# Split matrix products that stream the columns of each moving tile in chunks of 16, taken in turn from its two halves

## The chip, the cores and the metric

The kernel runs on one core of one Trainium2 chip. The metric is the device time of one execution in microseconds. Of the kernel before there are three timed runs, 2678.69, 2678.70 and 2680.71 us, so its median is 2678.7 us. One further execution was recorded by the hardware profiler; it took 2682.11 us, of which 2680.3 us lie between its first and its last instruction (its span). All rows below are of that execution.

## What is computed

Two transformer blocks in fp32, on 512 latent tokens (and 256 context tokens in the first block) of width 1024. Cut to the dense products, which are what the change touches:

```python
# first block, once
hx = modulate(rms_norm(x), sh1, sc1); hc = modulate(rms_norm(ctx), csh1, csc1)
... = split_cols(hx @ w_in)                  # 1024 x 7712; the context takes its first 3616 columns
... attention over 768 keys; a gated delta rule in both directions over chunks of 64 ...
x = x + g1 * ((sigmoid(g_a) * (attn @ w_pa) + sigmoid(g_d) * (gdn @ w_pd)) @ w_out)
x = x + g2 * conv_ffn(...)                   # w_up 1024 x 5632, w_down 2816 x 1024
# second block, twice
proj = rms_norm_2(h, norm1_g[l]) @ w_in[l]   # 1024 x 2576
... pool mixer, differential attention, gated linear attention ...
h = h + mix @ w_out[l]
h = h + square(relu(rms_norm_2(h, norm2_g[l]) @ w_mlp1[l])) @ w_mlp2[l]   # 1024 x 4096 x 1024
return rms_norm_2(h, final_norm_g)
```

## The kernel before

**Layout.** Activations lie with the feature on the partition and the token along the row: `KD` = 8 tiles of 128 features, each 512 columns wide (`LAT`) or 768 (`TOK`, with the context). A product gives 128 output features by 512 tokens, which fill one bank of PSUM, in fp32.

**Split products.** Each dense product is made of three products of "fp32r" operands, a high part and the rest: high x high, low x high and high x low. So a weight unit of 8 x 128 rows by 128 columns gives 24 TensorE matmuls into one bank, each with a weight load (LDWEIGHTS) of its own and a moving operand of 512 columns. Three pieces of code issue them. `product` (L321) streams the activations and holds the weights; for 768 tokens it issues two matmuls for each step, of 512 and of 256 columns. `product_tok` (L331) holds a tile of activations and streams the weights, 256 or 512 columns. `part` in `stage_mixer` (L2696) is `product` cut so that other work can go between. In the rows, `ps<-u_hi,w_lo` names the moving operand first and the stationary one behind it; the tiles `u`, `mid`, `h`, `h_lat`, `src`, `attn_back` and `gdn_o` are such pairs.

**Other TensorE work.** Attention, the delta rule, transposes and the small mixers use plain fp32 matmuls. The compiler makes two instructions of one such matmul; the table and the rows count instructions.

**Weights.** SyncE loads units of 512 KB into a ring of 4 in the order of their use (`stream_weights`). ScalarE copies a unit to `w_hi` (L291), VectorE subtracts it from the unit into `w_lo` (L299), two slots each. TensorE's `unit()` waits for `w_lo`; `unit_used` gives a slot back.

**Order.** Each stage has one hand-written program per engine, in a fixed order. TensorE works a product's unit from k = 0 to 7 in one go and turns over four banks (`n % 4`), so that ScalarE and VectorE can empty one while the next is filled.

**Alignment.** A tile of 512 elements or more starts at a multiple of 512 bytes in its row (`ROW`); so does the weight tile of each k, which is 128 columns of 4 bytes.

Of the kernel before, what the change touches and what calls it, by code (L numbers as in the profile page):

```python
# [25 lines left out]
P = 128  # L26
# [21 lines left out]
NCH = LAT // GLA_C  # L48
RING = 4
ROW = 512  # L50
UNIT = 8 * P
MOD_FIRST = 16
BIG = -1.0e30
# [109 lines left out]
def build(nc, t_vecs, t_mats, t_tabs, t_rope, t_x, t_w, out):  # L163

    with ExitStack() as top:
        signals = {}

        def sig(name):
            if name not in signals:
                signals[name] = Signal(top.enter_context(nc.semaphore(name)))  # L170
            return signals[name]
# [13 lines left out]
        def start_of(shape):  # L185

            return ROW if int(np.prod(shape)) >= ROW else 32

        def sb(ctx, name, *shape):

            taken[name] = taken.get(name, 0) + 1
            name = name if taken[name] == 1 else f"{name}_{taken[name]}"
            return ctx.enter_context(nc.sbuf_tensor(name, [P, *shape], F32, align_bytes=start_of(shape)))

        def sbr(ctx, name, *shape):
            taken[name] = taken.get(name, 0) + 1
            name = name if taken[name] == 1 else f"{name}_{taken[name]}"
            return ctx.enter_context(nc.sbuf_tensor(name, [P, *shape], F32R, align_bytes=start_of(shape)))

        def far_pair(ctx, name, *shape):  # L200

            taken[name] = taken.get(name, 0) + 1
            return tuple(ctx.enter_context(nc.sbuf_tensor(f"{name}_{part}{taken[name]}", [P, *shape], F32R, side="right",
                                                          align_bytes=ROW))
                         for part in ("hi", "lo"))
# [6 lines left out]
        mod = sb(top, "mod", 48, 2)  # L212
        ring = sb(top, "ring", RING, UNIT)
        w_hi, w_lo = sbr(top, "w_hi", 2, UNIT), sbr(top, "w_lo", 2, UNIT)
        tabs = sb(top, "tabs", NTAB)
        vecs = sb(top, "vecs", NVEC)
        ps = top.enter_context(nc.psum_tensor("ps", [P, 8, 512], F32))
# [84 lines left out]
        def unit(pe):  # L302

            n = at["used"]
            at["used"] += 1
            if whole[n]:
                pe.wait_ge(loaded[n % RING], 16 * (n // RING + 1))
                return ring[:, n % RING, :]
            pe.wait_ge(lo_ok.sem, n_split[n] + 1)
            return w_hi[:, n_split[n] % 2, :], w_lo[:, n_split[n] % 2, :]  # L310

        def pair(n):
            return ps[:, 2 * (n % 4):2 * (n % 4) + 2, :].rearrange("p b n -> p (b n)")

        def product(pe, w, src, dst, n_tok, k0=0, nk=KD, start=True, stop=True):

            for k in range(nk):
                for wi, xi in ((0, 0), (0, 1), (1, 0)):
                    for a, b in ((0, min(n_tok, LAT)), (LAT, n_tok)):
                        if a < b:  # L320
                            mm = nc.tensor.matmul(dst[:, a:b], w[wi][:, k * P:(k + 1) * P],  # L321
                                                  src[xi][:, k0 + k, a:b], start=start and k == wi == xi == 0,
                                                  stop=stop and k == nk - 1 and wi == 1)
            return mm

        def product_tok(pe, w, src, dst_of, n_tiles, cols, k0=0, nk=KD, start=True, stop=True):

            for t in range(n_tiles):
                for k in range(nk):
                    for xi, wi in ((0, 0), (0, 1), (1, 0)):  # L330
                        mm = nc.tensor.matmul(dst_of(t), src[xi][:, k0 + k, t * P:(t + 1) * P],  # L331
                                              w[wi][:, k * cols:(k + 1) * cols],
                                              start=start and k == wi == xi == 0,
                                              stop=stop and k == nk - 1 and xi == 1)
            return mm
# [13 lines left out]
        def stage_modulation(x, h, scratch, sq_scratch, spare):  # L349
# [22 lines left out]
            with stage_block() as block:  # L372
# [60 lines left out]
                def _(pe):  # L433
# [38 lines left out]
                    for k in range(KD):  # L472
                        pe.wait_ge(*h_low.at(k + 1))
                        mm = product(pe, tuple(p[:, k * P:(k + 1) * P] for p in w), h, pair(0), TOK, k0=k, nk=1,
                                     start=k == 0, stop=k == KD - 1)
# [127 lines left out]
        def product_of_norm(pe, w, src, dst, first=1):  # L603

            low = sig("norm_low")
            for k in range(KD):
                pe.wait_ge(*low.at(k + first))
                mm = product(pe, tuple(p[:, k * P:(k + 1) * P] for p in w), src, dst, LAT, k0=k, nk=1,
                             start=k == 0, stop=k == KD - 1)
            return mm  # L610
# [30 lines left out]
        def stage_attn_inputs(h, q, kk, vtok, spare, t1, rope, q_ss):  # L641
# [9 lines left out]
            with ExitStack() as s:  # L651
                sq, root = (spare[:].rearrange("p t n -> p (t n)")[:, a * 2 * TOK:(a + 1) * 2 * TOK]
                            .rearrange("p (b n) -> p b n", b=2) for a in range(2))
                with stage_block() as block:
# [6 lines left out]
                    def _(pe):  # L661
                        pe.wait_ge(*sig("tabs_rest").at(0))
                        for a in range(2):
                            w = unit(pe)
                            product_tok(pe, w, h, lambda t: ps[:, 2 + t, 0:KV_HEADS * P], TT, KV_HEADS * P, k0=4 * a,
                                        nk=4, start=a == 0, stop=a == 1).then_inc(*unit_used.one())
                        for n in range(n_items + 2):
                            if 0 < n < n_items:
                                w = unit(pe)
                                pe.wait_ge(*evac.at(max(n, 2)))  # L670
                                product(pe, w, h, pair(n % 2), items[n][1]).then_inc(*unit_used.one())
# [1897 lines left out]
        def stage_mixer(layer, u, x, first_gain, rstd, mats, mix):  # L2569
# [37 lines left out]
            def bank(n):  # L2607
                return n if n < 3 else (n - HEAD) % 2
# [18 lines left out]
            with ExitStack() as s:  # L2627
# [33 lines left out]
                with stage_block() as block:  # L2661
# [27 lines left out]
                    def _(pe):  # L2689
                        def part(w, n, k0, k1):  # L2690

                            for k in range(k0, k1):
                                if n == 0:
                                    pe.wait_ge(*sig("norm_low").at(k + 1 - KD))
                                for wi, xi in ((0, 0), (0, 1), (1, 0)):
                                    mm = nc.tensor.matmul(ps[:, bank(n), :], w[wi][:, k * P:(k + 1) * P], u[xi][:, k, :],  # L2696
                                                          start=k == wi == xi == 0, stop=k == KD - 1 and wi == 1)
                            if k1 == KD:
                                mm.then_inc(*unit_used.one())
# [107 lines left out]
                        for n in range(3):  # L2807
                            w = unit(pe)
                            pe.wait_ge(*evac.at(n - 3))
                            part(w, n, 0, KD)  # L2810
                            if n == 0:
                                pe.wait_ge(*lam_ok.at(1))
                                nc.tensor.matmul(ps[:, 7, 0:2], ones, lam[:, 0:2], start=True,
                                                 stop=True).then_inc(*lams_ok.one())
                        pe.wait_ge(*rs_ok.at(1))
                        for t in range(TL):
                            mm = nc.tensor.transpose(ps[:, 3, t * P:(t + 1) * P], rstd[:, t * P:(t + 1) * P], ident)
# [3 lines left out]
                                         start=True, stop=True).then_inc(*p_ok.one())  # L2821
                        pe.wait_ge(*lame_ok.at(1))
                        for i in range(2):
                            w = unit(pe)
                            product_tok(pe, w, u, lambda t: ps[:, 4 + t, 0:256], TL, 256,
                                        k0=4 * i, nk=4, start=i == 0, stop=i == 1).then_inc(*unit_used.one())
                        pe.wait_ge(*evac.at(3))
                        pe.wait_ge(*rc_ok.at(1))
                        for i in range(4):
                            w = unit(pe)  # L2830
                            for t in range(TL):
                                if i == 0 and t > 1:
                                    pe.wait_ge(*tok_evac.at(t - 1))
                                mm = product_tok(pe, w, tuple(a[:, :, t * P:(t + 1) * P] for a in u),
                                                 lambda _: ps[:, (2, 3, 6, 7)[t], :], 1, 512, k0=2 * i, nk=2,
                                                 start=i == 0, stop=i == 3)
                            mm.then_inc(*unit_used.one())
                            if i == 1:
                                pe.wait_ge(*d_ok.at(9))
                                for t in range(TL):  # L2840
                                    mm = nc.tensor.transpose(ps[:, 0, t * P:(t + 1) * P], ke[:, t * P:(t + 1) * P], ident)
# [6 lines left out]
                            elif i == 3:  # L2848
                                pe.wait_ge(*d_ok.at(11))
                                gla_states()  # L2850
                        pe.wait_ge(*d_ok.at(13))
                        part(unit(pe), HEAD, 0, KD)
                        w = unit(pe)
                        part(w, HEAD + 1, 0, 2)
                        pe.wait_ge(*d_ok.at(20))
                        pe.wait_ge(*tok_evac.at(8))
                        gla_out()
                        part(w, HEAD + 1, 2, KD)
                        for s in range(SLOTS):
                            n = FIRST + s  # L2860
                            ending, starting = items_ending(s), items_starting(s)
                            w = unit(pe)
# [472 lines left out]
        with ExitStack() as s:  # L3335
# [37 lines left out]
            u = far_pair(normed, "u", KD, LAT)  # L3373
# [8 lines left out]
            for layer in range(DEPTH2):  # L3382
                with ExitStack() as s2:
# [4 lines left out]
                    u = far_pair(normed, "u", KD, LAT)  # L3388
# [135 lines left out]
```

## Time and profile before

| | us |
|---|---|
| median of 3 runs | 2678.7 |
| profiled execution | 2682.1 |
| its span | 2680.3 |
| PE (matmul) busy | 2577.4 |
| PEld (weight load) busy | 2081.2 |
| VectorE busy | 1399.7 |
| ScalarE busy | 1023.4 |
| GpSimd busy | 277.2 |

A matmul's recorded time holds its way through the array as well as its streaming, and neighbours overlap: one of 512 columns is shown with 0.39 us while the next starts 0.23 us behind it. What a matmul costs in a dense run is therefore read from start to start. The granted clock is 1.00 for 2.4 GHz and 0.50 for 1.2 GHz; its mean in this execution is 0.975.

### The profile page before, as it was taken

Reading aid. Unit: us, or ns where it says so; the run is one execution under the profiler, and the core shown is the slowest. Engines: PE = TensorE matmul, PEld = TensorE weight load, DVE = VectorE, ACT = ScalarE, POOL = GpSimd, SP = SyncE. Lnnn points to the kernel's source line nnn. Section 1 sums busy time; section 2 is a strip of 40 time slices with the busy share of each in tenths; the row PEclk is TensorE's granted clock in tenths of the full one; section 3 lists DMA queues with packets and bytes.
Section 4 is the critical chain, followed back from the end, with each engine's and each line's share of the span. In section 5 each row is a group of like instructions: output and inputs, shape, how many; then the busy total and the mean of one; then the engine's idle time right before and its main releaser. Section 6 shows DMA issues by size and latency. Waiting matters only on the chain.

```text
span 2680.3 us, 46124 instructions
## 1 busy us (share of the span) xinstructions
PE 2577.4 (96%) x19758; PEld 2081.2 (78%) x19758; DVE 1399.7 (52%) x1950; ACT 1023.4 (38%) x1697; POOL 277.2 (10%) x228
## 2 busy tenths in 40 slices
PE   6998999999998999899999999999999999999998
PEld 5755787778987788688888877788888876788887
DVE  4345698545677433566653546553453446552542
ACT  3245665423334322333333436432233346431222
POOL 0210102223331000111101001100001001100001
PEclk8999999979999999999999989999999999999999
DMA  6100310131003233222323211233232211223322
GB/s 263 57 16 20 114 56 33 65 128 66 4 4 134 86 101 104 101 95 95 98 93 100 87 56 48 79 102 95 95 101 96 87 48 48 95 94 99 98 95 71
DMA packets 64715, 222.91 MB, mean 83 GB/s; under 512 B 7168, under 2 KB 7552, under 8 KB 64384
## 3 DMA queue, kind: packets, MB, share of 16 engines
q1 hardware_dynamic: 63936, 218.39, 24.3%
q8 instruction: 157, 2.57, 0.4%
q10 hardware_dynamic: 576, 1.57, 0.1%
q14 instruction: 46, 0.38, 0.0%
HBM read 213.64 MB, written 6.29 MB: 82 GB/s over the span
## 4 chain that ended last, share of the span: by engine, by line
PE 89%; DVE 6%; issue 2%; ACT 2%; DMA 1%; POOL 0%; SPq 0%; POOLq 0%; DVEq 0%; ACTq 0%
PE ps L321 59%; PE ps L2696 6%; PE ps L1715 5%; PE ps L331 3%; PE ps L837 2%; PE ps L812 1%; PE ps L1721 1%; PE ps L1740 1%; PE ps L1757 1%; DMA ring<-in_w_mod_first 1%; PE ps L2747 1%; DVE w_lo L299 1%; PE ps L828 1%; PE ps L2777 1%; PE ps L1915 1%
## 5 line engine op out<-in xcount | busy, mean ns | idle before, releaser
L299 DVE TENSOR_TENSOR w_lo<-ring,w_hi 128x1024 fp32r<-128x1024 f32 (+1 forms) x339 | 420.7, 1241 | 835.3 <-ACT w_hi L291 835.2
L291 ACT CAST w_hi<-ring 128x1024 fp32r<-128x1024 f32 (+1 forms) x339 | 353.9, 1044 | 922.1 <-PE ps L321 832.2
L321 PE MATMUL ps<-u_hi,w_hi 128*128 128x512 f32 x864 | 338.7, 392 | 9.0 <-DVE u_lo L580 9.0
L321 PE MATMUL ps<-u_hi,w_lo 128*128 128x512 f32 x864 | 336.9, 390 | 0.0
L321 PE MATMUL ps<-u_lo,w_hi 128*128 128x512 f32 x864 | 336.9, 390 | 0.0
L321 PE MATMUL ps<-mid_hi,w_hi 128*128 128x512 f32 x688 | 267.6, 389 | 0.0
L321 PE MATMUL ps<-mid_lo,w_hi 128*128 128x512 f32 x688 | 267.6, 389 | 0.0
L321 PE MATMUL ps<-mid_hi,w_lo 128*128 128x512 f32 x688 | 267.6, 389 | 0.0
L321 PEld LDWEIGHTS ps<-u_hi,w_hi 128*128 128x128 f32 x864 | 162.5, 188 | 46.8 <-issue 8.9
L321 PEld LDWEIGHTS ps<-u_hi,w_lo 128*128 128x128 f32 x864 | 162.6, 188 | 34.0
L321 PEld LDWEIGHTS ps<-u_lo,w_hi 128*128 128x128 f32 x864 | 162.6, 188 | 33.8 <-issue 0.5
L2371 POOL TENSOR_TENSOR project_acc<-project_acc,project_sq 128x512 f32<-128x512 f32 x42 | 54.0, 1292 | 1140.2 <-ACT project_sq L2392 1140.2
L321 PEld LDWEIGHTS ps<-mid_hi,w_lo 128*128 128x128 f32 x688 | 129.1, 188 | 26.9
L321 PEld LDWEIGHTS ps<-mid_hi,w_hi 128*128 128x128 f32 x688 | 129.1, 188 | 26.8
L321 PEld LDWEIGHTS ps<-mid_lo,w_hi 128*128 128x128 f32 x688 | 129.1, 188 | 26.8
L321 PE MATMUL ps<-h_hi,w_hi 128*128 128x512 f32 (+1 forms) x432 | 139.5, 380 | 3.7 <-ACT gdn_v L709 2.6
L321 PE MATMUL ps<-h_lo,w_hi 128*128 128x512 f32 (+1 forms) x432 | 129.3, 357 | 0.3 <-issue 0.3
L321 PE MATMUL ps<-h_hi,w_lo 128*128 128x512 f32 (+1 forms) x432 | 128.9, 356 | 0.0
L2696 PE MATMUL ps<-u_hi,w_hi 128*128 128x512 f32 x240 | 104.2, 434 | 0.0
L2696 PE MATMUL ps<-u_hi,w_lo 128*128 128x512 f32 x240 | 95.7, 399 | 0.0
L2696 PE MATMUL ps<-u_lo,w_hi 128*128 128x512 f32 x240 | 95.3, 397 | 0.0
L321 PEld LDWEIGHTS ps<-h_hi,w_hi 128*128 128x128 f32 x432 | 72.2, 191 | 22.2 <-DVE w_lo L299 5.9
(449 smaller groups left out, 4677.5 us busy)
## 6 DMA issues: line engine op xcount, KB each, us to landing
ring<-in_w_up SPq DMA_DIRECT2D x44, 512.0 KB, 3.4
ring<-in_w_in SPq DMA_DIRECT2D x42, 512.0 KB, 3.5
ring<-in_w_merge SPq DMA_DIRECT2D x32, 512.0 KB, 3.5
ring<-in_w_mlp1a SPq DMA_DIRECT2D x32, 512.0 KB, 3.5
ring<-in_w_mlp2a SPq DMA_DIRECT2D x32, 512.0 KB, 3.5
ring<-in_w_mlp1b SPq DMA_DIRECT2D x32, 512.0 KB, 3.5
ring<-in_w_mlp2b SPq DMA_DIRECT2D x32, 512.0 KB, 3.5
ring<-in_w_gdn_in SPq DMA_DIRECT2D x24, 512.0 KB, 3.5
```

What stands on the lines that cost most here:

```text
L291: nc.scalar.copy(w_hi[:, slot, 0:width], ring[:, n % RING, 0:width]).then_inc(*hi_ok.one())
L299: nc.vector.tensor_tensor(w_lo[:, slot, 0:width], ring[:, n % RING, 0:width], as_f32(w_hi[:, slot, 0:width]), ALU.subtract).then_inc(*lo_o ...
L321: mm = nc.tensor.matmul(dst[:, a:b], w[wi][:, k * P:(k + 1) * P], src[xi][:, k0 + k, a:b], start=start and k == wi == xi == 0, stop=stop a ...
L331: mm = nc.tensor.matmul(dst_of(t), src[xi][:, k0 + k, t * P:(t + 1) * P], w[wi][:, k * cols:(k + 1) * cols], start=start and k == wi == xi ...
L812: mm = nc.tensor.matmul(pair(i % 2)[:, a:b], q[:, h, t * P:(t + 1) * P], kk[:, h // GROUP, a:b], start=True, stop=True)
L828: mm = nc.tensor.transpose(pt_bank[:, k * P:(k + 1) * P], pr[:, i % 2, k * P:(k + 1) * P], ident)
L837: mm = nc.tensor.matmul(ps[:, 6, :], vtok[:, k, c:c + P], pt[:, k, :], start=k == 0, stop=k == TT - 1)
L1715: mm = nc.tensor.matmul(dst[:, h * P:(h + 1) * P], lhs(h), rhs(h), start=True, stop=True)
L1721: mm = nc.tensor.transpose(dst[:, h * P:(h + 1) * P], src(h), ident)
L1740: mm = nc.tensor.matmul(packed(y_bank(d)[r, h * B32 // 2:(h + 1) * B32 // 2], 2 << lev), n_block(n, d, h, r, r), joined(up[r, d, h * B32:( ...
L2371: nc.gpsimd.tensor_tensor(acc[:, i, :], acc[:, i, :], sq[:, i, n % 2, :], ALU.add).then_inc(*add_ok.one())
L2696: mm = nc.tensor.matmul(ps[:, bank(n), :], w[wi][:, k * P:(k + 1) * P], u[xi][:, k, :], start=k == wi == xi == 0, stop=k == KD - 1 and wi ...
```

## The change

```diff
+LINE = 16
...
+        def halves(a):
+            return a.rearrange("p (half l c) -> p l half c", half=2, c=LINE)
+
         def product(pe, w, src, dst, n_tok, k0=0, nk=KD, start=True, stop=True):
...
-                            mm = nc.tensor.matmul(dst[:, a:b], w[wi][:, k * P:(k + 1) * P],
-                                                  src[xi][:, k0 + k, a:b], start=start and k == wi == xi == 0,
+                            mm = nc.tensor.matmul(halves(dst[:, a:b]), w[wi][:, k * P:(k + 1) * P],
+                                                  halves(src[xi][:, k0 + k, a:b]), start=start and k == wi == xi == 0,
...
-                        mm = nc.tensor.matmul(dst_of(t), src[xi][:, k0 + k, t * P:(t + 1) * P],
-                                              w[wi][:, k * cols:(k + 1) * cols],
+                        mm = nc.tensor.matmul(halves(dst_of(t)), src[xi][:, k0 + k, t * P:(t + 1) * P],
+                                              halves(w[wi][:, k * cols:(k + 1) * cols]),
...
-                                    mm = nc.tensor.matmul(ps[:, bank(n), :], w[wi][:, k * P:(k + 1) * P], u[xi][:, k, :],
+                                    mm = nc.tensor.matmul(halves(ps[:, bank(n), :]), w[wi][:, k * P:(k + 1) * P],
+                                                          halves(u[xi][:, k, :]),
```

The moving operand of a 512-column matmul was read as columns 0 to 511. Now it is read as 0-15, 256-271, 16-31, 272-287 and so on, 32 chunks; one of 256 columns as 0-15, 128-143, 16-31 and so on, 16 chunks. The output goes to the same columns of PSUM in the same order, so each sum lands where it did. The stationary operand, its load, the number and order of the instructions, waits, DMAs and all other engines are as before.

TensorE, at the border of the projection behind the first block's merge and the stage of `w_up` (`src` and `u` are split activations, `project_acc` and `project_sq` sums for a norm), before:

```order
L321 MATMUL ps<-src_hi_buf,w_hi 128x512
L321 MATMUL ps<-src_lo_buf,w_hi 128x512
L321 MATMUL ps<-src_hi_buf,w_lo 128x512
L2358 MATMUL ps<-project_acc,tabs 128x512
L2361 MATMUL ps<-project_sq,tabs 128x512
L2489 UNCONDITIONAL_BRANCH
L321 MATMUL ps<-u_hi,w_hi 128x512
L321 MATMUL ps<-u_lo,w_hi 128x512
L321 MATMUL ps<-u_hi,w_lo 128x512
```

and now:

```order
L325 MATMUL ps<-src_hi_buf,w_hi 128x16x2x16
L325 MATMUL ps<-src_lo_buf,w_hi 128x16x2x16
L325 MATMUL ps<-src_hi_buf,w_lo 128x16x2x16
L2362 MATMUL ps<-project_acc,tabs 128x512
L2365 MATMUL ps<-project_sq,tabs 128x512
L2493 UNCONDITIONAL_BRANCH
L325 MATMUL ps<-u_hi,w_hi 128x16x2x16
L325 MATMUL ps<-u_lo,w_hi 128x16x2x16
L325 MATMUL ps<-u_hi,w_lo 128x16x2x16
```

The split matmuls read 16 x 2 x 16 columns where they read 512; the two plain ones and the order stand as they were (the lines are four further down).

TensorE, in `product_tok` of the mixer of the second block, where the moving operand is the weights, before:

```order
L331 MATMUL ps<-w_hi,u_hi 128x256
L331 MATMUL ps<-w_lo,u_hi 128x256
L331 MATMUL ps<-w_hi,u_lo 128x256
L331 MATMUL ps<-w_hi,u_hi 128x512
L331 MATMUL ps<-w_lo,u_hi 128x512
L331 MATMUL ps<-w_hi,u_lo 128x512
```

and now:

```order
L335 MATMUL ps<-w_hi,u_hi 128x8x2x16
L335 MATMUL ps<-w_lo,u_hi 128x8x2x16
L335 MATMUL ps<-w_hi,u_lo 128x8x2x16
L335 MATMUL ps<-w_hi,u_hi 128x16x2x16
L335 MATMUL ps<-w_lo,u_hi 128x16x2x16
L335 MATMUL ps<-w_hi,u_lo 128x16x2x16
```

Here too only the shape is another: 8 x 2 x 16 for 256 columns, 16 x 2 x 16 for 512.

## Rows read from the trace of the kernel before

**Rows 1.** The page: engines' busy time, and the chain by engine and by line.

```profile
PE 2577.4 (96%) x19758; PEld 2081.2 (78%) x19758; DVE 1399.7 (52%) x1950; ACT 1023.4 (38%) x1697; POOL 277.2 (10%) x228
...
PE 89%; DVE 6%; issue 2%; ACT 2%; DMA 1%; POOL 0%; SPq 0%; POOLq 0%; DVEq 0%; ACTq 0%
PE ps L321 59%; PE ps L2696 6%; PE ps L1715 5%; PE ps L331 3%; PE ps L837 2%; PE ps L812 1%; PE ps L1721 1%; PE ps L1740 1%; PE ps L1757 1%; DMA ring<-in_w_mod_first 1%; PE ps L2747 1%; DVE w_lo L299 1%; PE ps L828 1%; PE ps L2777 1%; PE ps L1915 1%
```

**Rows 2.** The chain in order of time: start us, us, what (long pieces).

```profile
1138.15 355.48 PE ps L321 x1566
...
1612.73 1.39 PE ps L2696 x6
...
1733.24 348.22 PE ps L321 x1536
```

**Rows 3.** Busy PE in the whole span of L321, L331, L2696: us, us (count), clock.

```profile
0.00:2681.00 2681.00, 1687.33 (x7488) 0.98 0.25 83
...
0.00:2681.00 2681.00, 85.71 (x528) 0.98 0.25 83
...
0.00:2681.00 2681.00, 188.65 (x720) 0.98 0.25 83
```

**Rows 4.** Groups by form: the three products of `h` have 256-column forms, 152 each.

```profile
L321 PE MATMUL ps<-h_hi,w_hi 128*128 128x256 f32 x152 | 43.1, 283 | 0.0
...
L331 PE MATMUL ps<-w_hi,u_hi 128*128 128x512 f32 x64 | 25.3, 396 | 0.0
```

**Rows 5.** Timeline of PE, full clock: start us, us, engine, line, operation.

```profile
1859.82 0.39 PE L321 MATMUL ps<-mid_lo,w_hi 128*128 128x512 f32 x1
...
1865.94 0.39 PE L321 MATMUL ps<-mid_lo,w_hi 128*128 128x512 f32 x1
```

**Rows 6.** The same, at half clock, shortly after a wait.

```profile
1690.87 0.63 PE L321 MATMUL ps<-src_hi_buf,w_lo 128*128 128x512 f32 x1
...
1692.58 0.63 PE L321 MATMUL ps<-src_hi_buf,w_hi 128*128 128x512 f32 x1
```

**Rows 7.** The same, plain fp32 at full clock: a run cut after 5 and after 7; L1715.

```profile
179.44 2.41 PE L837 MATMUL ps<-o_tok,gdn_v 128*128 128x512 f32 x5 [0.89 <-ACT o_tok L881]
...
179.44 3.27 PE L837 MATMUL ps<-o_tok,gdn_v 128*128 128x512 f32 x7 [0.89 <-ACT o_tok L881]
...
646.93 1.06 PE L1715 MATMUL ps<-gdn_St,gdn_k 128*128 128x128 f32 x8
```

**Rows 8.** All of L837: ns min/median/max, first and last start.

```profile
L837 PE MATMUL ps<-o_tok,gdn_v x96: 592/592/697, 164.7 to 272.0; 128*128 128x512 f32 x96
```

**Rows 9.** Timeline: 256 columns alone, and 512 and 256 in pairs (x2).

```profile
58.04 0.28 PE L331 MATMUL ps<-w_lo,h_hi 128*128 128x256 f32 x1
...
58.76 0.28 PE L331 MATMUL ps<-w_lo,h_hi 128*128 128x256 f32 x1
...
351.50 0.51 PE L321 MATMUL ps<-h_hi,w_lo 128*128 128x512 f32 x2
...
352.54 0.51 PE L321 MATMUL ps<-h_hi,w_lo 128*128 128x512 f32 x2
...
411.61 0.51 PE L321 MATMUL ps<-h_hi,w_lo 128*128 128x512 f32 x2
...
415.85 0.40 PE L321 MATMUL ps<-h_hi,w_lo 128*128 128x512 f32 x1
```

**Rows 10.** Groups by form: small matmuls of 16 columns each, mean ns of one.

```profile
L1757 PE MATMUL ps<-gdn_y,gdn_t 32*32 32x16 f32 x3072 | 35.5, 182 | 0.4 <-DVE gdn_y L1458 0.4
...
L1740 PE MATMUL ps<-gdn_u,ring 32*32 32x16 f32 x2560 | 30.9, 182 | 4.0 <-issue 2.3 <-DVE gdn_u L1494 1.7
```

**Rows 11.** Who waited for whom; then VectorE's busy time in dense stretch and mixer.

```profile
ACT w_hi L291 <- PE ps L321: 832.2, 278, 10.7
...
1140.00:1490.00 350.00, 190.17 (x234) 1.00 0.30 97
...
1551.00:1689.00 138.00, 77.77 (x138) 0.95 0.14 46
```

## The prediction, made before the changed kernel ran

> **What bounds the kernel now.** I read the page's busy times and its chain first. TensorE is busy 96% of the span and makes up 89% of the chain; the three lines that issue split products (L321, L2696, L331) are 59, 6 and 3% of it [rows 1]. The chain in order of time then shows how clean these stretches are: one piece of 1566 matmuls in 355.48 us, another of 1536 in 348.22 us, with nothing between [rows 2]. So in two thirds of the span the time is a count of matmuls times the step from one start to the next, and everything hangs on what sets that step.
>
> 348.22 / 1536 is 226.7 ns, and the timeline of such a stretch says the same: 27 steps from 1859.82 to 1865.94 make 226.7 ns [rows 2, 5]. 512 columns at 2.4 GHz are 213.3 ns. 13.4 ns of each step are therefore not streaming. Three comparisons say what they may be.
> - A split matmul of 256 columns takes steps of 0.72 / 6 = 120 ns [rows 9], again 13.3 ns more than its 106.7. The extra belongs to a matmul with its weight load, not to the columns.
> - At half clock it is gone: four steps from 1690.87 to 1692.58 are 427.5 ns [rows 6], and 512 / 1.2 is 426.7.
> - In plain fp32 at full clock two instructions of 512 columns add 0.86 us, 430 ns each [rows 7]. That is 1024 array cycles (426.7 ns) and about 2.3 to 3 ns more, although each has its weight load too.
>
> What the last two share is the pace of the moving operand. A load that cannot hide costs 697 - 592 = 105 ns for 128 columns [rows 8], 1.2 columns per ns. At half clock, and in plain fp32 where a column takes two array cycles, the moving operand also passes at 1.2 columns per ns; in a split product at full clock it passes at 2.4 beside the same load. The stall is there only where the one runs twice as fast as the other. That it depends on how the two meet, and is no fixed price of a swap, is shown by the pairs of 512 and 256 columns: the same work takes 1.04 / 3 = 347 ns a pair in one unit and 4.24 / 12 = 353 in another [rows 9].
>
> **My reading of the change.** While 128 columns of weights (512 bytes) are read, a full-speed stream reads 256 columns, 1024 bytes. If the memory's parts repeat at 512 bytes or less along a row (not shown by any row; all these tiles begin at multiples of 512 bytes), the stream overtakes the load once per load, however long the matmul is, and waits for about 16 columns of weights: 105 / 128 x 16 = 13.1 ns, near the 13.3 found. With chunks of 16 taken in turn from two halves (1024 bytes apart, or 512 for 256 columns) the stream moves on by 16 columns of its half for every 32 it streams: the pace of the load. Then a split matmul is in the case of plain fp32, with no overtaking.
>
> **The sum.** Nothing is added or removed in number: instructions, waits, DMAs, the other engines' work and all queues stand as before, and no wait moves. Only the step changes.
> - Counts: L321 has 7488 matmuls, L331 528, L2696 720 [rows 3]. 3 x 152 of L321 have 256 columns, and 3 x 64 of L331 have 512 [rows 4]. That gives 7944 of 512 columns, 456 of them in pairs with one of 256, and 336 of 256 columns alone.
> - 512 alone (7488): new step 213.3 + 2.3 = 215.6 ns, the 2.3 from plain fp32 [rows 7]; saved 11.0 ns each, 82.4 us.
> - 256 alone (336): the nearest row is plain fp32 of 128 columns, which also streams for 256 array cycles: (1.06 - 0.28) / 7 = 111.5 ns [rows 7, 9]. Saved 8.5 ns each, 2.9 us.
> - Pairs (456): now 347 to 353, say 350; then 215.6 + 111.5 = 327.1. Saved 22.9 each, 10.4 us.
> - At half clock there is nothing to save. The clock's mean of 0.975 (0.98 in [rows 3]) means 5% of the time at half speed, so near 3% of the matmuls: 95.7 x 0.97 = 92.8 us.
> - On the path: the three lines are 68% of 2680, 1823 us; all split matmuls at their steps are 7944 x 0.2267 + 792 x 0.12 = 1896 us. 96% of them lie on the chain: 89 us.
> - What is late next: in a dense stretch VectorE is busy 190 of 350 us, and ScalarE's 278 waits before a weight copy last 832.2 us, 3.0 us each [rows 11]. A unit of 24 matmuls gets 24 x 11 = 264 ns shorter, which this wait takes up; no one else becomes the bound. In the mixers products go in groups of six (1.39 us, [rows 2]) between other work, and VectorE is busy 78 of 138 us [rows 11]; there I count off a quarter of 720 x 11 ns, 2 us.
>
> Sum: 87 us. The profiled execution takes 2682.1 us, 3.4 above the median of 2678.7; taken from each, 2595 for a profiled one and **2592 for the median**.
>
> **Bounds of the step.** Below, 213.3 and 106.7 ns with no overhead at all: 7488 x 13.4 + 456 x 30 + 336 x 13.3 = 118 us, x 0.97 x 0.96 = 110, so 2569. Above, the stall kept in full and a price for the 32 chunks on top, which no dense row shows; its size is taken up under the third case.
>
> **The rivals.**
> *The order makes no difference.* Weight load and stream may share a way out of the memory, where each piece of weights takes a turn from the stream whatever its address: with 13.3 ns per load at full speed, and turns to spare when the stream needs half as many, it explains the same three comparisons. For it: the long pieces of the chain have the same step, 227.0 and 226.7 ns [rows 2], whatever tiles they read. Against it: the pairs' 347 and 353. It gives 2679, within 3 us. The Trainium skill (TensorE: Matmul & The Clock Gate, "What happens when you issue a matmul", step 1) says that TensorE has two independent read ports, so that loading the next weights takes nothing from the running matmul. By that rule too the order would gain nothing, and the same page's N / 2.4 + 2.5 ns for a warm step would be 215.8; the trace has 226.7 and does not agree, so the rule weighs little here.
>
> *Each chunk costs something.* Reading and writing in 32 pieces may cost at every jump. The price: one array cycle, 0.42 ns, is 13.3 ns per 512 columns and 6.7 per 256. With the stall gone, a step of 215.6 + 13.3 = 228.9 against 226.7 loses 2.2 ns, 7488 times, less about 3 ns won per pair: +14 us, 2693. With the stall still there it is 7944 x 13.3 + 792 x 6.7 = 111 us, on the path +103: 2782. It decides from 11.0 / 32 = 0.34 ns per chunk. Against it: the small products at L1740 read and write 16 columns in runs of 2 to 16 and take 182 ns in the mean, as do those of L1757, which write one run [rows 10]; yet 16 columns lie under their weight load, so these rows would hide a cycle per jump. The Trainium skill (Advanced Engine Details and Errata, "Memory Cachelines") says that any non-contiguous pattern in PSUM slows matmuls significantly, and in the same place that every two consecutive elements should be contiguous; by the first sentence this case is the likely one, by the second runs of 16 are free. No figure stands there, and no row here has a dense run of such writes.
>
> *Half of the gain.* If the new order only makes the meetings rarer, the step ends between, near 221 ns: -45 us, 2634. I count it with the forecast's own range.
>
> **How the numbers follow.** The step as in plain fp32, whole or in part: 0.60, own range 2569 to 2635. No difference: 0.16. Slower: 0.24, of which 0.10 up to 2700 and 0.14 beyond. The likeliest case gives the time, 2592. The range from 2569 to 2700 leaves out 0.14 above and a few hundredths below. A measurement of this kernel tells some 0.2%, 5 us, from no change; the cases lie well apart by that: faster 0.60, same 0.16, slower 0.24.
>
> **What would show it.** In the dense stretches of the changed kernel the step from start to start is the whole answer: near 215.6 ns, the forecast (1536 matmuls in 331 us); 226.7, the second case; above 226.7, the third. Steps of 256 columns near 111.5 and pairs near 327 would show that the size of each term was right, and at half clock 427 must stay: more than that there, and the chunks cost by themselves. ScalarE's wait before the weight copy should shrink by some 0.3 us a unit. The forecast is wrong if the stall is bound to the load alone, if a jump costs over 0.34 ns, or if the mixers' other engines take back what TensorE gives.

## The result: 3.5% slower

The changed kernel takes 2776.6 us (four runs, 2765.2 to 2782.1) against 2679.7 us; the ratio is 1.0351, with a 95% interval of 1.0314 to 1.0388. The forecast was 2592 us, and the range up to 2700 does not hold the time. The profiled execution has a span of 2780.2 us, at a mean clock of 0.979.

The page of the changed kernel, engines' busy time and the chain, beside [rows 1]:

```profile
PE 2684.5 (97%) x19758; PEld 2106.5 (76%) x19758; DVE 1398.7 (50%) x1950; ACT 1023.6 (37%) x1697; POOL 276.9 (10%) x228
...
PE 90%; DVE 6%; issue 2%; ACT 2%; DMA 1%; POOL 0%; SPq 0%; POOLq 0%; DVEq 0%; ACTq 0%
```

TensorE alone has more to do, 107 us of it; VectorE, ScalarE and GpSimd are where they were. Its chain in order of time (start us, us, what), beside [rows 2]:

```profile
1160.11 376.28 PE ps L325 x1566
...
1782.50 368.65 PE ps L325 x1536
```

The same 1536 matmuls take 368.65 us where they took 348.22: 240.0 ns a step in place of 226.7. The timeline shows how even it is, beside [rows 5]; then the half-clock steps beside [rows 6], matmuls of 256 columns alone and pairs of 512 and 256 beside [rows 9]:

```profile
1859.86 0.40 PE L325 MATMUL ps<-u_hi,w_lo 128*128 128x512 f32 x1
...
1862.26 0.40 PE L325 MATMUL ps<-u_hi,w_hi 128*128 128x512 f32 x1
```

```profile
1152.06 0.63 PE L325 MATMUL ps<-u_lo,w_hi 128*128 128x512 f32 x1
1152.49 0.63 PE L325 MATMUL ps<-u_hi,w_lo 128*128 128x512 f32 x1
```

```profile
58.04 0.28 PE L335 MATMUL ps<-w_hi,h_lo 128*128 128x256 f32 x1
...
58.76 0.28 PE L335 MATMUL ps<-w_hi,h_lo 128*128 128x256 f32 x1
```

```profile
359.61 0.52 PE L325 MATMUL ps<-h_lo,w_hi 128*128 128x512 f32 x2
...
361.77 0.52 PE L325 MATMUL ps<-h_lo,w_hi 128*128 128x512 f32 x2
```

Ten steps are 2.40 us, 240 ns. At half clock a step is still 0.43 us: there the new order costs nothing. 256 columns alone still take 0.72 / 6 = 120 ns, and a pair 2.16 / 6 = 360 ns where it took 347 to 353. The loss is thus in the 512-column matmuls at full clock: 7488 x 13.3 ns and 456 x 10 ns are 104.2 us. By their start times and the granted clock only 93 of the 8736 split matmuls began at half clock before, and 79 now. That is some 1%, where the prediction took 3%. With 0.99 for the clock and the prediction's 0.96 for the path the sum is 99.0 us; measured are 96.9. The four runs lie 17 us apart, so nothing finer can be read from this agreement, but no second loss is needed.

### The profile page after: what moved, and what is told of

The parts are those of the page before. It is cut to its first block, busy times and chain, and to the rows that moved or that the text cites. A ratio compares the mean times of both kernels' runs of the same rounds, so it can differ in the third digit from the quotient of the medians.

```text
span 2780.2 us, 46124 instructions
## 1 busy us (share of the span) xinstructions
PE 2684.5 (97%) x19758; PEld 2106.5 (76%) x19758; DVE 1398.7 (50%) x1950; ACT 1023.6 (37%) x1697; POOL 276.9 (10%) x228
## 4 chain that ended last, share of the span: by engine, by line
PE 90%; DVE 6%; issue 2%; ACT 2%; DMA 1%; POOL 0%; SPq 0%; POOLq 0%; DVEq 0%; ACTq 0%
PE ps L325 61%; PE ps L2700 6%; PE ps L1719 5%; PE ps L335 3%; PE ps L841 2%; PE ps L1744 1%; PE ps L816 1%; PE ps L1725 1%; PE ps L1761 1%; PE ps L2752 1%; PE ps L1919 1%; PE ps L2782 1%; PE ps L832 1%; DMA ring<-in_w_mod_first 1%; PE ps L2755 1%
## 5 line engine op out<-in xcount | busy, mean ns | idle before, releaser
L292 ACT CAST w_hi<-ring 128x1024 fp32r<-128x1024 f32 (+1 forms) x339 | 352.8, 1041 | 1011.9 <-PE ps L325 916.3
L325 PE MATMUL ps<-u_hi,w_hi 128*128 128x512 f32 x864 | 350.8, 406 | 8.3 <-DVE u_lo L584 8.3
L325 PE MATMUL ps<-u_lo,w_hi 128*128 128x512 f32 x864 | 348.8, 404 | 0.0
L325 PE MATMUL ps<-u_hi,w_lo 128*128 128x512 f32 x864 | 348.8, 404 | 0.0
L325 PE MATMUL ps<-mid_hi,w_lo 128*128 128x512 f32 x688 | 277.0, 403 | 0.0
L325 PE MATMUL ps<-mid_hi,w_hi 128*128 128x512 f32 x688 | 277.0, 403 | 0.0
L325 PE MATMUL ps<-mid_lo,w_hi 128*128 128x512 f32 x688 | 277.0, 403 | 0.0
L2700 PE MATMUL ps<-u_hi,w_hi 128*128 128x512 f32 x240 | 106.7, 445 | 0.0
L2700 PE MATMUL ps<-u_lo,w_hi 128*128 128x512 f32 x240 | 98.3, 410 | 0.0
L2700 PE MATMUL ps<-u_hi,w_lo 128*128 128x512 f32 x240 | 98.3, 410 | 0.0
```

Of the source, the lines that this page charges most:

```text
L292: nc.scalar.copy(w_hi[:, slot, 0:width], ring[:, n % RING, 0:width]).then_inc(*hi_ok.one())
L325: mm = nc.tensor.matmul(halves(dst[:, a:b]), w[wi][:, k * P:(k + 1) * P], halves(src[xi][:, k0 + k, a:b]), start=start and k == wi == xi == 0,
L2700: mm = nc.tensor.matmul(halves(ps[:, bank(n), :]), w[wi][:, k * P:(k + 1) * P], halves(u[xi][:, k, :]), start=k == wi == xi == 0, stop=k = ...
```

## The experiments

A stage here is one dense stretch of the program that works one product, and a step is the time from one matmul's start to the next one's. Steps given to a tenth of a ns are means over the steps of a stage at full clock, without the few of 260 ns and more that hold a wait, from the start times in the trace. The rows shown are windows of 70 us in such a stage with the count of matmuls in them; beside a known step they are easily read: 310 or 311 matmuls are 226.7 ns, 302 are 233, 298 are 237, 293 are 240, 290 are 243 and 282 are 250.

The first four kernels ran four or ten times each and are judged by their times. Each of the others ran once and has several orders in it, one to a stage, so its time (2729.1, 2704.6, 2702.5, 2894.9, 2702.5, 2686.9 and 2732.4 us for e5 to e11) says little, and only the steps within its stages are compared. The edits are shortened; a line in plain words stands for the code that picks each stage's setting.

### Reading or writing

```diff
-mm = nc.tensor.matmul(halves(dst[:, a:b]), ...          # all three places
+mm = nc.tensor.matmul(in_order(dst[:, a:b]), ...        # e1: PSUM written in column order
```
```diff
-    halves(src[xi][:, k0 + k, a:b])
+    in_order(src[xi][:, k0 + k, a:b])                   # e2: moving operand read in column order
```

> Only the moving operand is read in the new order; PSUM is written in column order, so the output's columns are permuted and the numbers are not the reference's. The changed kernel's step is 240.0 ns for 512 columns (64 array cycles over 512) and 120.0 for 256 (32 over 256): 2 cycles for each of the 32 or 16 chunks, and nothing else. If the price of a chunk is paid in the READING, the step stays at 240 and the time at 2777. If it is paid in the WRITING, the step falls: to 215.6 ns (time near 2592) if the new reading order also takes the weight load's stall away, to 226.7 (2680) if it does nothing.

> Only PSUM is written in the new order; the moving operand is read in column order, so the output's columns are permuted and the numbers are not the reference's. Price in the READING: the step is the old 226.7 ns and the time 2680. Price in the WRITING: 240 ns or more (2777), up to 253 (2870) if the load's stall of 13.3 ns comes on top of 26.7 for the 32 chunks.

Measured: reading alone in chunks 2776.3 us, ratio 1.0369 (1.0337 to 1.0401); writing alone in chunks 2676.4 us, ratio 0.9995 (0.998 to 1.0009). The same piece of the chain, first of the one, then of the other:

```profile
1792.40 368.65 PE ps L327 x1536
```

```profile
1724.04 348.21 PE ps L327 x1536
```

368.65 us to the digit of the changed kernel, and 348.21 as before it. The whole cost is paid in reading the moving operand. Writing PSUM in 32 pieces of 64 bytes costs nothing that can be measured.

### Longer chunks

```diff
-LINE = 16
+LINE = 32      # e3;  e4: LINE = 64
```

> Chunks of 32 columns, read and written in turn from the halves: 16 chunks in 512 columns. If a chunk costs 2 array cycles (0.83 ns) and the stall beside the weight load is gone because the stream goes at the load's pace: 213.3 + 13.3 = 226.7 ns, 2680. If the load still needs its 32 cycles and only takes them out of the gaps between chunks that fall beside it (8 of the 16, 16 cycles): 512 + 32 - 16 + 32 = 560 cycles, 233 ns, 2730. If chunk and stall simply add: 240 ns, 2777.

> Chunks of 64 columns, 8 in 512. Stall gone: 213.3 + 6.7 = 220 ns, 2630. Load fed out of the gaps beside it (4 chunks, 8 cycles): 512 + 32 - 8 + 16 = 552 cycles, 230 ns, 2705. Both added: 233 ns, 2730.

Measured: chunks of 32 2744.3 us, ratio 1.0258 (1.0228 to 1.0288); chunks of 64 2678.4 us, ratio 1.0002 (0.9982 to 1.0021). The piece of 1536 in the first and in the second:

```profile
1757.85 363.53 PE ps L325 x1536
```

```profile
1739.88 348.22 PE ps L325 x1536
```

236.7 ns and 226.7 ns a step. None of the three sums expected fits either: from 16 to 32 columns the number of jumps halves and 3.3 of 13.3 ns go, from 32 to 64 it halves again and the other 10 go. So it is no price per jump on top of a fixed stall, and with chunks of 64 the stream is no faster than in column order although it too keeps the load's mean pace.

### Other distances and lengths

```diff
+def visit(x):    # way = (A, B, C), set for each stage; source and PSUM alike
+    return x.rearrange("p (a b c) -> p b a c", a=at["way"][0], b=at["way"][1])
```

> The old order everywhere but in nine stages, each with an order of its own, PSUM written in the same one; a stage is read by its step (columns 512, old 226.7 ns). A, B, C stands for B turns of A chunks of C columns, where the A chunks of a turn lie 512 / A columns apart. Two theories. PLACE: what costs is to read again too soon the place of the memory just read, and places repeat along a row; so the distance of a jump decides, not the number. COUNT: each jump costs about the same, 0.83 ns, and the load is fed in the gaps. first down projection 2,16,16 (as in the change): 240 for both. Second block, layer 0: 4,8,16 (jumps of 512 bytes): PLACE 253 if places repeat at 512 bytes or less (24 of 32 chunks follow one at the same place, against 16 of 32 now), 226.7 if they repeat only at 1024; COUNT 240. 8,4,16 (256 bytes): PLACE 260 if they repeat at 256, else 226.7; COUNT 240. 16,2,16 (128 bytes): PLACE 226.7 or less, COUNT 240. 2,32,8 (chunks of 8): PLACE 240 if the place is 16 columns wide, more if it is narrower; COUNT 267. Layer 1: 8,2,32 and 4,4,32 (chunks of 32, 256 and 512 bytes apart): COUNT 237 for both, as measured for 32; PLACE different ones. 2,2,128: both 226.7. 2,64,4: COUNT 320; PLACE 240 to 320.

The windows, in the order of the program: old order; 2,16,16; 4,8,16; 8,4,16; 16,2,16; 2,32,8; 8,2,32; 4,4,32; 2,2,128; 2,64,4 (from, to, us, busy PE and its count, clock, DMA share, GB/s):

```profile
1145.00:1215.00 70.00, 70.00 (x310) 1.00 0.31 98
1385.00:1455.00 70.00, 70.00 (x293) 1.00 0.29 90
1755.00:1825.00 70.00, 70.00 (x304) 1.00 0.30 95
1845.00:1915.00 70.00, 70.00 (x294) 1.00 0.28 90
1935.00:2005.00 70.00, 70.00 (x293) 1.00 0.29 90
2025.00:2095.00 70.00, 70.00 (x290) 1.00 0.29 90
2358.00:2428.00 70.00, 70.00 (x298) 1.00 0.30 94
2448.00:2518.00 70.00, 70.00 (x302) 1.00 0.30 97
2540.00:2610.00 70.00, 70.00 (x310) 1.00 0.31 98
2630.00:2700.00 70.00, 70.00 (x282) 1.00 0.21 68
```

| columns in a chunk | jumps of | step, ns |
|---|---|---|
| 512 (old), 128 | none, 1024 bytes | 226.7, 226.7 |
| 32 | 1024 (e3), 256, 512 bytes | 236.7, 236.6, 233.3 |
| 16 | 1024, 128, 256, 512 bytes | 240.0, 240.0, 239.4, 231.2 |
| 8 | 1024 bytes | 243.3 |
| 4 | 1024 bytes | 250.0 |

COUNT falls: 128 jumps cost 23 ns and 32 jumps 13. PLACE falls too, in the form expected: where four chunks in a row lie 512 bytes apart the step is the best of its length and not the worst. The distance does play a part, but I have no rule that gives these numbers. Source and PSUM were visited alike in all these stages. That PSUM's part is free was measured only for chunks of 16 from two halves, so for the other ways it is not shown which side pays.

### Is the 13.3 ns of the old order the weight load?

```diff
+m = way's M for low x high and high x low, else P
-mm = nc.tensor.matmul(dst[:, a:b], w[wi][:, k * P:(k + 1) * P], ...
+mm = nc.tensor.matmul(visit(dst[0:m, a:b], c), w[wi][:, k * P:k * P + m], ...
```

> In ten stages the low x high and high x low products load fewer columns of weights (M) and so compute only M of 128 output features, which leaves part of the computation out. Stages as (M, chunk; 0 is the old order): up (64, 0), first down (32, 0); second block, layer 0: (64, 16), (32, 16), (96, 0), (32, 32); layer 1: (128, 0), (128, 16), (32, 64), (64, 64). Read is the step of a matmul during which the next load has M columns. If the load causes the 13.3 ns, M = 96, 64 and 32 give 223, 220 and 217 ns in the old order. In the changed order: if the 26.7 ns belong to the stream alone (a chunk that follows one at the same place), 240 stays for M = 32; if they are load and stream together, it falls to 233 for M = 64 and 230 or less for M = 32. Chunks of 64 should go with the old order.

Groups of weight loads (mean ns behind the bar); then the windows of the stages (32, 0), (32, 16), (32, 32) and (128, 0):

```profile
L328 PEld LDWEIGHTS ps<-mid_lo,w_hi 128*32 128x32 f32 x432 | 46.9, 109 | 19.9
L328 PEld LDWEIGHTS ps<-mid_lo,w_hi 128*128 128x128 f32 x128 | 24.3, 190 | 6.4
```

```profile
1385.00:1455.00 70.00, 70.00 (x305) 1.00 0.30 95
...
1835.00:1905.00 70.00, 70.00 (x293) 1.00 0.28 90
...
2015.00:2085.00 70.00, 70.00 (x298) 1.00 0.28 91
...
2341.00:2411.00 70.00, 70.00 (x311) 1.00 0.30 97
```

The loads became 80 ns shorter, and the steps did not fall: 229 to 231 ns beside loads of 32 columns, 227 to 232 beside 64, 233 beside 96, against 226.7 with full loads. They even rose a little, in no order of the size. Chunks of 16 have 240.0 beside loads of 32, 64 and 128 columns; chunks of 32 beside loads of 32 have 236.0. This falsifies my reading: less to load does not make the stream faster, neither in the old order nor in the new. No run has a stream without any load beside it, so a small price that each load has whatever its size is not ruled out.

### How the step grows with the width

```diff
-for a, b in ((0, min(n_tok, LAT)), (LAT, n_tok)):
+for a, b in way's widths, inner k only:
+    mm = nc.tensor.matmul(dst[0:m, a:b], w[wi][:, k * P:k * P + m], ...
```

> In ten stages the inner k of a unit (all but the first and the last) issue their 512 columns in several matmuls, each with a load of its own, and the low x high and high x low products load M columns of weights (M = 64 or 32 leaves part of the computation out). Stages as (M, widths): up (128, 256 256), first down (32, 256 256); second block, layer 0: (32, 384 128), (32, 128 x4), (128, 384 128), (32, 64 x8); layer 1: (128, 128 x4), (64, 448 64), old, (64, 192 320). After 7 units of small loads: if the extra belongs to each matmul whatever its width (a start of 16 half-speed cycles of the fetch), N columns take N / 2.4 + 13.3 ns where the load is short: 384 173, 256 120, 128 67, 64 40. If it grows with the columns from some length on, or with the load, the small ones come out otherwise: 128 columns at 53 + 3 = 56 if there is no start price. With full loads 128 columns should be bound by the load, 107 to 120 ns.

Timelines of stages of this kernel (x4 and x2 are the pieces of one 512-column product): (32, 128 x4), then (32, 256 256), and last, with full loads, (128, 128 x4) and (128, 256 256):

```profile
1900.46 0.41 PE L326 MATMUL ps<-mid_lo,w_hi 128*32 128x128 f32 x4
1900.70 0.40 PE L326 MATMUL ps<-mid_hi,w_lo 128*32 128x128 f32 x4
1900.94 0.61 PE L326 MATMUL ps<-mid_hi,w_hi 128*128 128x128 f32 x4
```

```profile
1400.03 0.40 PE L326 MATMUL ps<-mid_hi,w_hi 128*128 128x256 f32 x2
1400.26 0.40 PE L326 MATMUL ps<-mid_lo,w_hi 128*32 128x256 f32 x2
1400.50 0.40 PE L326 MATMUL ps<-mid_hi,w_lo 128*32 128x256 f32 x2
```

```profile
2499.80 0.61 PE L326 MATMUL ps<-u_lo,w_hi 128*128 128x128 f32 x4
2500.24 0.61 PE L326 MATMUL ps<-u_hi,w_lo 128*128 128x128 f32 x4
```

```profile
1199.84 0.40 PE L326 MATMUL ps<-u_hi,w_lo 128*128 128x256 f32 x2
...
1200.80 0.40 PE L326 MATMUL ps<-u_hi,w_hi 128*128 128x256 f32 x2
```

Beside loads of 32 columns, 128 columns take 60.0 ns (0.24 / 4), 256 take 117.5, 384 take 174.4, and 512 some 230.4 (the kernel above). Less the pure streaming that is 6.7, 10.8, 14.4 and 17 ns: about 3 ns for each matmul and 3.6 for each 128 columns. The extra does grow with the columns.

With full loads 128 columns take 110.9 ns (0.44 / 4): they are held by the load, since beside a short one they take 60.0. 256 columns take 119.8 (0.96 / 8), only 2.3 more than beside short loads. So most of the 120 ns of [rows 9] is the stream's own price; whether the load adds the 2.3 is not shown. That 256 columns and 512 columns had the same extra of 13.3 ns with full loads was chance: beside short loads it is 10.8 and 17.

### Where load and stream begin

```diff
-w[wi][:, k * P:(k + 1) * P]
+w[wi][:, k * P + shift:(k + 1) * P + shift]                     # e6, e10: k < 7
-src[xi][:, k0 + k, a:b]
+src row from column (k0 + k) * LAT + shift                      # e9, e10
```

> The old order of columns. In ten stages the weight tile of k < 7 begins some columns further in its row (4 bytes each): up 2, first down 1; second block, layer 0: 16, 32, 48, 64, layer 1: 80, 96, 8, 4. The weights are the wrong ones there, so the numbers are not the reference's. If the stall of 13.3 ns is a meeting of load and stream at the same place of the memory, it depends on where in the 512 bytes the load begins against the stream: the steps differ between the stages (222 to 235 ns). If each piece of the load simply takes a turn from the stream, every stage with a shift of a multiple of 4 columns (16 bytes) has 226.7 ns; an uneven start may cost one piece more (227.1).

> The old order of columns. In ten stages the moving tile of most k begins some columns further (the values are the wrong ones, so the numbers are not the reference's): up 2, first down 1; second block, layer 0: 16, 32, 48, 64, layer 1: 128, 256, 8, 4 columns of 4 bytes. If what counts is where the load begins against the stream, shifts of the stream give what shifts of the weights gave (16, 32, 48, 8, 4: 229 to 233 ns; 64: 226.7), with 128 and 256 at 226.7. If the weight tile has to begin at a multiple of 256 bytes for a reason of its own, all these have 226.7. Besides, attention's plain fp32 products read and write in chunks: the scores in chunks of 4 columns, the products with v in chunks of 16. If the gaps between chunks are lost only where the array takes a column every 0.42 ns, these stay at 429 ns for 512 columns; if they are lost at any pace, the products with v take 456 ns.

> The old order of columns. In ten stages the weight tile and the moving tile of k < 7 both begin the same number of columns further (wrong values, so the numbers are not the reference's): up 16, first down 32; second block, layer 0: 16, 32, 48, 8, layer 1: 4, 2, 1, 64. Shifting only the one gave 229 to 233 ns for 16, 32, 48 and 8, and 226.7 for 64. If what counts is how load and stream lie to each other, all stages fall back to 226.7. If each has to begin at a multiple of 256 bytes, they stay at 229 to 237, and only 64 has 226.7.

First the weights shifted alone, by 16, 32, 48 and 64 columns; then both, by 16, 32, 48, 8, 4, and by 1:

```profile
1750.00:1820.00 70.00, 70.00 (x302) 1.00 0.28 90
1840.00:1910.00 70.00, 70.00 (x302) 1.00 0.29 91
1930.00:2000.00 70.00, 70.00 (x308) 1.00 0.31 98
2016.00:2086.00 70.00, 70.00 (x311) 1.00 0.31 96
```

```profile
1740.00:1810.00 70.00, 70.00 (x308) 1.00 0.32 98
1826.00:1896.00 70.00, 70.00 (x309) 1.00 0.31 97
1914.00:1984.00 70.00, 70.00 (x308) 1.00 0.32 98
2002.00:2072.00 70.00, 70.00 (x308) 1.00 0.31 98
2325.00:2395.00 70.00, 70.00 (x303) 1.00 0.29 91
...
2505.00:2575.00 70.00, 70.00 (x297) 1.00 0.30 91
```

| shift, columns | weights | stream | both |
|---|---|---|---|
| 16 | 232.8 | 231.2 | 228.1, 228.1 |
| 32 | 232.8 | 232.7 | 227.6, 227.6 |
| 48 | 228.6 | 233.0 | 228.5 |
| 64 | 226.7 | 226.7 | 226.7 |
| 128, 256 | | 226.8, 226.7 | |
| 80, 96 | 232.8, 232.8 | | |
| 8 | 232.8 | 233.2 | 228.9 |
| 4, 2 | 233.1, 230.7 | 231.9, 232.5 | 232.4, 232.2 |
| 1 | 232.4 | 237.2 | 236.7 |

So load and stream do meet. Where only one of the two is moved, the step is 226.7 for multiples of 64 columns (256 bytes), and for the rest mostly 231 to 233; moving the weights by 48 costs least, 228.6, and the stream by 1 most, 237.2. If both are moved alike by 8 to 48 columns, most steps are 226.7 again: those of the 8th to the 20th matmul in a unit of 24. The mean is a little higher because k = 7, the last three of a unit, was not shifted, and the steps around it are uneven.

To begin at the same place modulo 256 bytes is not enough by itself. Both moved alike by 4, 2 and 1 columns (16, 8 and 4 bytes) stay at 232.4, 232.2 and 236.7. Of the starts tried those at multiples of 32 bytes have the good step, and those at 16 bytes or less from one do not. The kernel before, with all its tiles at multiples of 512 bytes, was already in the best of these states nearly everywhere.

That kernel of shifted streams also held attention's plain fp32 products in chunks. The chain's pieces of twelve and eleven of them:

```profile
195.75 5.42 PE L846 MATMUL ps<-o_tok,gdn_v 128*128 128x512 f32 x12 [0.89 <-ACT o_tok L890]
210.43 4.99 PE L846 MATMUL ps<-o_tok,gdn_v 128*128 128x512 f32 x11 [0.89 <-ACT o_tok L890]
```

The difference is 0.43 us for one, as in [rows 7], and the scores in chunks of 4 columns have 429 ns as before. At this pace of a column every second array cycle (429 ns are 1030 cycles for 512 columns) neither of the two kinds of chunks costs anything.

### Chunks and the load together

```diff
+c, shift = at["way"]
+matmul(visit(dst, c), w[wi][:, k * P + shift:(k + 1) * P + shift], visit(src, c), ...
```

> Chunks taken in turn from the two halves, and the weight tile of k < 7 moved some columns (wrong values for a shift, so the numbers are not the reference's). Stages as (chunk, shift): up (16, 64), first down (16, 32); second block, layer 0: (32, 0), (32, 16), (32, 32), (32, 64); layer 1: (64, 0), (64, 32), (128, 0), (8, 0). If chunks of 16 cost by the stream alone, (16, 64) and (16, 32) stay at 240.0 ns. If the 237 of chunks of 32 is a chance meeting with the load, a shift changes it by several ns; if not, 237 for all four. Chunks of 64 and 128 should go as the old order: 226.7, and near 233 with a shift of 32. Chunks of 8: 243.

The stages (16, 32), (32, 0), (32, 16), (64, 0) and (64, 32):

```profile
1405.00:1475.00 70.00, 70.00 (x294) 1.00 0.29 90
1770.00:1840.00 70.00, 70.00 (x297) 1.00 0.28 90
1860.00:1930.00 70.00, 70.00 (x298) 1.00 0.29 91
...
2370.00:2440.00 70.00, 70.00 (x311) 1.00 0.31 96
2458.00:2528.00 70.00, 70.00 (x304) 1.00 0.29 93
```

Chunks of 16 stay at 240.0 with a shift of 64 and of 32, chunks of 32 at 236.6 to 236.7 with all four shifts, chunks of 8 at 243.3. Chunks of 64 go with the old order, 226.8 and, with a shift of 32, 231.7; chunks of 128 have 226.7. In chunks of 16 or 32 the step does not depend on where the load begins, and no place brings back the 226.7 of the old order, whose other places give 232. The 13.3 ns of the change can therefore be read as two parts of like size: the good meeting with the load, which is lost, and some 8 ns from 232 to 240.0 that come with the short chunks themselves. That it is two parts and that they add is my reading of these numbers, not shown.

## Why the prediction was wrong, point by point

**What bounds the kernel** was right. Two thirds of the span are matmuls times their step, no other engine stepped in, and the new step times the counts gives 99.0 us for the measured 96.9. ScalarE's wait before the weight copy, which was to shrink by 0.3 us a unit, grew by it: 916.3 us in 278 waits where it had 832.2.

**The step that failed** is the first of the three comparisons: "The extra belongs to a matmul with its weight load, not to the columns". It rested on 120 ns for 256 columns, read as 106.7 + 13.3. With short loads 256 columns take 117.5, 128 take 60.0 and 512 take 230.4, so the extra grows with the columns and does not shrink with the load. A row of a second width is a weak second point where another limit sits close by; [rows 7] had that limit, 111.5 ns, and I used it only for the new step.

Two steps of the forecast fell with it. To move at the load's pace was to take the stall away: chunks of 64 do so too and have 226.7, the old step, and 231.7 with the load moved by 32 columns, as the old order has some 232. So the pace alone gains nothing. And the forecast's sum held no term for reading in chunks, without a row that said so: reading alone in chunks of 16 costs 13.3 ns a step. The condition that places repeat at 512 bytes or less along a row did hold: as far as the shifts show, the meeting of load and stream repeats every 256 bytes.

**The other two comparisons** (no extra at half clock, next to none in plain fp32) were right as rows and hold in the changed kernel too, where neither pays for chunks. But two mechanisms explain them alike: a stream that meets a load of another pace, and a stream that by itself is at the limit of what can be read for it. I took the first. Loads of a quarter of the size, which gain nothing, speak for the second, but do not show it. There is a meeting too, shown by the shifts, and the pairs' 347 and 353 may come from something like it, which no run tested. It is worth 6 ns between its good and its usual state, and the kernel had the good one. Of this the change had nothing to win.

**The term of the sum.** "Saved 11.0 ns each" for 512 columns was in truth 13.3 lost; 8.5 for 256 alone was 0; 22.9 for a pair was 10 lost. The share at half clock, taken from the mean over the whole span as 3%, was 1%.

**The rivals.** *The order makes no difference* is out for reading, and right for PSUM. The Trainium skill's rule that the load takes nothing from the running matmul (TensorE: Matmul & The Clock Gate, "What happens when you issue a matmul") agrees with this case in that a smaller load frees nothing, 227 to 233 ns beside small loads and 226.7 beside full ones. As to the load's place it does not: 226.7 against some 232. *Each chunk costs something* was the case that came. Its upper price, one array cycle for each of 32 chunks with the old extra kept, gave 2782 for the measured 2776.6, by luck. Its form was wrong: 256 columns pay nothing, longer chunks do not pay in proportion, and the chunks cost in the reading, where I had set the Trainium skill's sentence on PSUM beside it. That sentence of the Trainium skill (Advanced Engine Details and Errata, "Memory Cachelines": any non-contiguous pattern slows matmuls significantly) does not hold for runs of 64 bytes: ratio 0.9995. The other one of the Trainium skill there, that every two consecutive elements should be contiguous, agrees with it.

**The chances.** I gave this case 0.24 and its part above 2700 us 0.14. What argued against it, the small products of [rows 10], was called weak in the same sentence, since they run under their loads; they are plain fp32 besides, which paid for no jump in the chunks tried. No row of a dense full-clock stream spoke against a price, so little stood behind the 0.60 but one mechanism inferred from coincidences of 13.3 and 13.1 ns.

**Still open**: what part of the read path makes chunks below 64 columns dear, why jumps of 512 bytes cost less than those of 128, 256 or 1024, and why a step beside short loads lies some 3 ns and 3.6 ns per 128 columns above the pace of 2.4 GHz.

## What to carry to other kernels

Where TensorE streams fp32r operands at one column per cycle, let the moving operand be read in runs of at least 64 columns (256 bytes), and let the weight tile and the moving tile begin at the same place modulo 256 bytes, on a multiple of 32 bytes. PSUM may be written in runs of 16 columns from two halves. At half clock and in plain fp32, where a column takes two cycles, the chunks tried cost nothing; shifts were not tried there. Before a mechanism is built on an extra that looks constant, take widths that no other limit touches, and change the size of the supposed cause.

## What was not expected of the hardware

- The moving operand's order alone decides: 240.0 ns when read in chunks of 16 columns, 226.7 when only PSUM is written so.
- Chunks of 4, 8, 16, 32 and 64 columns in turn from two halves, read and written: 250.0, 243.3, 240.0, 236.7 and 226.7 ns for 512 columns at 2.4 GHz. At half clock it is 427 in the old order and in chunks of 16, 32 and 64, and in plain fp32 429 in the old order and in chunks of 4 and 16.
- The place of the weight tile against the moving tile is worth some 6 ns a step, and a smaller load gains nothing: 226.7 ns beside 128 columns, 233.3, 229.5 and 230.4 in the mean of a stage where two loads of three have 96, 64 and 32.
- Split matmuls beside short loads: 60.0, 117.5, 174.4 and some 230.4 ns for 128, 256, 384 and 512 columns.
